# Gates of one token block added into DRAM by indirect transfers in place of one-hot products

## What is computed

```python
q = (h @ w_q).reshape(B, T, 8, 2, 128)               # 8 heads, two halves
s = einsum('bthpd,hpnd->bthpn', q, sub_keys)         # 128 keys for each half
v1, i1 = top_k(s[..., 0, :], 16); v2, i2 = top_k(s[..., 1, :], 16)
cand = v1[..., :, None] + v2[..., None, :]
top_s, pos = top_k(cand, 16)                         # 16 experts of 128*128 a head
eidx = i1 * 128 + i2 at pos
gates = softmax(top_s)
act = gelu(h . u_tab[eidx]);  out = sum(gates * act * v_tab[eidx])
```

## Time and profile before

| | |
|---|---|
| Three runs | 1858.15, 1858.62, 1856.65 us, median 1858.15 us |
| Profiled execution | span 1856.8 us from the first to the last instruction; no other time of it is listed |
| Busy | PE 95%, PEld 84%, DVE 70%, ACT 40%, POOL 41% of the span |
| Granted clock of TensorE | 0.981 of full speed on average |
| Transfers | 432.64 MB, 232 GB/s over the span |

### The profile page before, as it was taken

The page is one execution under the profiler, slowest core; times in us unless marked ns, Lnnn a source line. Parts: engine busy times, 40 slices in busy tenths (PEclk is TensorE's granted clock), DMA queues, the critical chain, the costliest instruction groups (busy, mean ns, idle before and its releaser), DMA issues. The chain is left out here.

```text
span 1856.8 us, 31058 instructions
## 1 busy us (share of the span) xinstructions
PE 1768.2 (95%) x11485; PEld 1564.7 (84%) x11485; DVE 1307.3 (70%) x2777; ACT 742.8 (40%) x1227; POOL 764.5 (41%) x449
## 2 busy tenths in 40 slices
PE   3999999999998989999999999879999999999998
PEld 2666888878877889999999999879998888888887
DVE  5993454553224679878869999756787888777777
ACT  4332332242234233333337767633333333333334
POOL 2333232344442448777753333122454443332330
PEclk9998999999999999999999999989999999999999
DMA  9661101022322249888868999978899999889883
GB/s 356 217 233 71 36 16 34 25 91 91 102 79 103 91 141 314 282 292 292 286 235 281 341 311 331 319 264 285 287 317 337 370 370 359 326 320 328 316 325 145
DMA packets 179267, 432.64 MB, mean 233 GB/s; under 512 B 15816, under 2 KB 91720, under 8 KB 179040
## 3 DMA queue, kind: packets, MB, share of 16 engines
q1 hardware_dynamic: 125088, 273.71, 42.5%
q0 software_dynamic: 36864, 134.23, 20.3%
q10 hardware_dynamic: 17216, 23.36, 3.4%
HBM read 383.54 MB, written 47.71 MB: 232 GB/s over the span
## 5 line engine op out<-in xcount | busy, mean ns | idle before, releaser
L201 POOL DMA_INDIRECT own_rows<-in_peer_v_dram,own_row x128 | 212.3, 1659 | 330.8 <-DVE y_own L2094 312.7
L1988 PE MATMUL banks<-v_hi,coef_lo 128*128 128x512 f32 x756 | 294.6, 390 | 0.0
L1988 PE MATMUL banks<-v_lo,coef_hi 128*128 128x512 f32 x756 | 294.5, 390 | 0.0
L1988 PE MATMUL banks<-v_hi,coef_hi 128*128 128x512 f32 x756 | 294.1, 389 | 0.1
L201 POOL DMA_INDIRECT own_rows<-in_u_rows_dram,own_row x128 | 160.6, 1255 | 233.1 <-DVE own_rows L1733 178.8
L2079 DVE TENSOR_TENSOR v_lo<-weight_ring,v_hi 128x1024 fp32r<-128x1024 f32 x128 | 156.5, 1222 | 24.7 <-ACT v_hi L2027 22.7
L1988 PEld LDWEIGHTS banks<-v_hi,coef_hi 128*128 128x128 f32 x756 | 142.0, 188 | 29.5 <-issue 0.5
L1988 PEld LDWEIGHTS banks<-v_hi,coef_lo 128*128 128x128 f32 x756 | 141.9, 188 | 29.5
L1988 PEld LDWEIGHTS banks<-v_lo,coef_hi 128*128 128x128 f32 x756 | 141.9, 188 | 28.9
L2094 DVE SCALAR_TENSOR_TENSOR y_own<-own_rows,own_coef,y_own 128x1024 f32<-128x1024 f32 x128 | 163.8, 1279 | 1.9 <-DVE y_own L2094 0.5
L1397 PE MATMUL banks<-h_hi,wring_hi 128*128 128x384 f32 (+2 forms) x448 | 155.2, 347 | 4.0 <-ACT gelu_early L1479 2.9
(11 more groups left out here) (393 smaller groups left out, 4346.1 us busy)
## 6 DMA issues: line engine op xcount, KB each, us to landing
weight_ring<-in_peer_v_dram SPq DMA_DIRECT2D x128, 512.0 KB, 5.4
weight_ring<-in_peer_u_dram SPq DMA_DIRECT2D x68, 512.0 KB, 4.5
ada<-in_w_ada_dram SPq DMA_DIRECT2D x48, 512.0 KB, 5.7
gate_scratch<-gate_block SPq DMA_DIRECT2D x48, 512.0 KB, 7.0
gate_tiles<-gate_scratch SPq DMA_DIRECT2D x32, 768.0 KB, 6.9
gelu_scratch<-gelu_early ACTq DMA_DIRECT2D x104, 192.0 KB
gelu<-gelu_scratch SPq DMA_DIRECT2D x104, 192.0 KB, 5.6
u_early<-in_peer_u_dram SPq DMA_DIRECT2D x36, 512.0 KB, 7.1
```

The lines of the kernel that those rows point to most:

```text
L201: pool.indirect_dma_start(own_rows[:, n % R], None, tables[n // NS], bass.IndirectOffsetOnAxis(ap=own_row[:, n % NS:n % NS + 1], axis=0)). ...
L1988: last = nc.tensor.matmul(y_bank(t, half)[:], w[:, j, t * P:(t + 1) * P], x[:, j, c], start=(first and n == 0), stop=False)
```

## The change

NSC = 1 of the three dense blocks no longer goes through one-hot products; only NHOT = 256 tokens do (HOT_TILES = 2), in NR = 4 turns. For the third block, VectorE works out for each head the 16 gates of a token (`list_gates`: softmax of that head alone, ScalarE's Exp by `add_exp`) and the place of each in the gates' DRAM tensor; GpSimd adds each into that place by an indirect transfer with 128 indices, one element of 4 bytes each (`add_gates`): 16 transfers a head, 128 in all. The tensor's part is zeroed before, by eight stores of SP in the DeltaNet stage. A head's adds wait until all of the head before have landed. Heads 0 to 5 are added during heads 2 to 7 of the search, two adds after each piece; heads 6 and 7 at the start of the one-hot stage, ahead of the fetches. In the search VectorE makes every second low part of the u pieces (`dve_split`), there are 4 dots a head, not 8, the loop over the heads is unrolled, and GpSimd fetches one row for two pieces. The expert stage has 36 u tiles, not 24, and 192 own rows, not 144.

```diff
+NSC = 1
+NHOT = TD - NSC * P
+HOT_TILES = NHOT // P
+NR = NHOT // (2 * TB)
-DOT_HEAD, DOT_ITER = 8, 8
+DOT_HEAD, DOT_ITER = 4, 8
-OWN_GELU = 8
+OWN_GELU = 22
+ZERO_PARTS = 8
...
-    if p < OWN_GELU:
-        return 2
-    if p == OWN_GELU:
-        return 0
+    if p < OWN_GELU - 1:
+        return 3
+    if p <= OWN_GELU:
+        return OWN_GELU - p
     if p < EXP_TILES - N_EARLY:
-        return 2 + (j > 0)
+        return 3
     if i >= 30:
         return int(j < 3)
-    return 0 if j == 0 else 1 if j < 3 else 1 + (i < 14)
+    return int(p > EXP_TILES - N_EARLY)
...
+                def add_gates(pool, h, n):
+                    if n == 0:
+                        pool.wait_ge(add_ready, h + 1)
+                        pool.wait_ge(gates_added, 16 * NSC * TOPK * h) if h else pool.wait_ge(gates_zeroed, 16 * ZERO_PARTS)
+                    t, k = n // TOPK, n % TOPK
+                    pool.indirect_dma_start(gates_at, bass.IndirectOffsetOnAxis(ap=add_at[:, h, t, k:k + 1], axis=0),
+                                            add_gate[:, h, t, k:k + 1], None, compute_op=ALU.add).then_inc(gates_added, 16)
...
                 nc.vector.memset(eps[:], EPS).then_inc(*V.step("eps"))
+                nc.vector.memset(g["zeros"][:], 0.0).then_inc(g["zeros_made"], 1)
...
+                    if i < ZERO_PARTS:
+                        sp.dma_start(spill[:, c, NHOT // TB:].rearrange("p g o j t -> p g (o j t)"),
+                                     g_["zeros"][:].unsqueeze(1).to_broadcast([P, EXP_TILES // G // ZERO_PARTS, NSC * G * P])).then_inc(g_["gates_zeroed"], 16)
...
+        def dve_split(n):
+            return n >= B0 + HR and (n - B0 - HR) % 2 == 1
...
+                def add_exp(h):
+                    act.wait_ge(*VB.after("add_shift", h))
+                    nc.scalar.activation(add_gate[:, h], add_gate[:, h], ACT.Exp).then_inc(add_exped, 1)
...
-                        if m == U_HEAD // 2 - 1 and h + 1 < PH:
-                            copy(h + 1)
+                        if m == U_HEAD // 2:
+                            if h + 1 < PH:
+                                copy(h + 1)
+                            if h:
+                                add_exp(h - 1)
+                add_exp(PH - 1)
...
-                n = R
-                for m in range(PH * U_HEAD):
-                    while n - R < (m + 1) * DOT_HEAD // U_HEAD:
-                        fetch(pool, n)
-                        n += 1
-                    if B0 + HR + m < NPIECE:
-                        rest(B0 + HR + m)
+                for h in range(PH):
+                    for m in range(U_HEAD):
+                        k = h * U_HEAD + m
+                        if k % 2:
+                            fetch(pool, R + k // 2)
+                        if B0 + HR + k < NPIECE and not dve_split(B0 + HR + k):
+                            rest(B0 + HR + k)
+                        if h >= 2:
+                            for n in range(m * NSC * TOPK // U_HEAD, (m + 1) * NSC * TOPK // U_HEAD):
+                                add_gates(pool, h - 2, n)
...
+                def list_gates(h):
+                    i1, i2 = (sel[:, n, SC, h, :] for n in range(2))
+                    total, inv, base, column = add_sum[:, 0], add_sum[:, 1], add_tmp[:, 0], add_tmp[:, 1]
+                    dve.wait_ge(add_exped, h + 1)
...
+                for h in range(PH):
+                    def fill(i):
+                        if i % 3 == 0:
+                            rest(B0 + HR + h * U_HEAD + 2 * (i // 3) + 1)
+                        if i in (1, 4, 7, 8):
+                            dot(h * DOT_HEAD + (1, 4, 7, 8).index(i))
+                        if i == 7 and h:
+                            list_gates(h - 1)
+                    topk(VB, h, DENSE, fill)
                 dve.wait_ge(*VB.after("sel1", PH - 1))
-                shift(VP, 0, ND)
-                softmax(VP, 0, ND, th(gates[:, 0:ND]), "gates")
+                shift(VP, 0, HOT_TILES)
+                list_gates(PH - 1)
+                softmax(VP, 0, HOT_TILES, th(gates[:, 0:HOT_TILES]), "gates")
...
                 pool.sem_inc(gelu_done, 2)
+                for h in (PH - 2, PH - 1):
+                    for n in range(NSC * TOPK):
+                        g_["add_gates"](pool, h, n)
                 for n in range(PH * DOT_HEAD + R, U_DONE + R):
                     fetch(pool, n)
```

More of the change, by code:

```diff
@@ L166, in program @@
             env["zT"] = sb(mix, "zT", [P, HJ, T])
+            env["zeros"] = sb(mix, "zeros", [P, NSC * G * P])
+            env["zeros_made"] = sem(mix, "zeros_made")
             env["scT"] = sb(mix, "scT", [P, HJ, T])
@@ L1457, in _ @@
                     pe.wait_ge(*(VB.after("sel1", PH - 1) if n < 2 else VP.after("gates")))
-                    for t in range(ND):
+                    for t in range(HOT_TILES):
                         src = (sel[:, n, t] if n < 2 else gates[:, t]).rearrange("p h k -> p (h k)")
@@ L1659, in _, with dot @@
                 dve.wait_ge(*VO.after("h_own"))
[L1661 to L1668 removed]
+                def dot(n):
+                    dve.wait_ge(row_landed[n % R], 16 * (n // R) + 16)
+                    nc.vector.scalar_tensor_tensor(rows[:, n % R], rows[:, n % R], 1.0, h_psum[:], ALU.mult, ALU.mult,
+                                                   accum_out=own_act[:, n:n + 1]).then_inc(row_used, 1)
@@ new lines, in rest @@
+                def rest(n):
+                    if n < NPIECE:
+                        dve.wait_ge(hi_ready, n + 1)
+                        nc.vector.tensor_tensor(w_lo[n % HR][:], w[:, n % WR], w_hi[n % HR][:].bitcast(F32), ALU.subtract).then_inc(lo_by_dve, 1)
+                def list_gates(h):
+                    i1, i2 = (sel[:, n, SC, h, :] for n in range(2))
+                    total, inv, base, column = add_sum[:, 0], add_sum[:, 1], add_tmp[:, 0], add_tmp[:, 1]
+                    dve.wait_ge(add_exped, h + 1)
+                    nc.vector.tensor_reduce(total, add_gate[:, h], AX.X, ALU.add).then_inc(*VS.step("sum"))
+                    dve.wait_ge(*VS.after("sum", h))
+                    nc.vector.reciprocal(inv, total).then_inc(*VS.step("inv"))
+                    nc.vector.tensor_copy(add_q[:], i2).then_inc(*VS.step("i2"))
+                    dve.wait_ge(*VS.after("i2", h))
+                    nc.vector.tensor_scalar(add_q[:], add_q[:], 2, None, ALU.logical_shift_right).then_inc(*VS.step("group"))
+                    for n in range(NSC):
+                        last = nc.vector.tensor_scalar(base[:, n], i1[:, n], float(ROW_P), lanes[:, n:n + 1], ALU.mult, ALU.add)
+                    last.then_inc(*VS.step("base"))
+                    dve.wait_ge(*VS.after("base", h))
+                    nc.vector.scalar_tensor_tensor(column, i2, float(TB), base, ALU.mult, ALU.add).then_inc(*VS.step("column"))
+                    dve.wait_ge(*VS.after("column", h))
+                    nc.vector.scalar_tensor_tensor(add_at[:, h], add_q[:], float(ROW_G - G * TB), column, ALU.mult, ALU.add).then_inc(*VS.step("at"))
+                    nc.vector.tensor_tensor(add_gate[:, h], add_gate[:, h], inv.unsqueeze(2).to_broadcast([P, NSC, TOPK]), ALU.mult).then_inc(*VS.step("gate"))
+                    dve.wait_ge(*VS.after("gate", h))
+                    dve.sem_inc(add_ready, 1)
@@ new lines, in _ @@
+                for n in range(NSC):
+                    nc.vector.tensor_scalar(lanes[:, n:n + 1], C["lane"][:, 0:1], float((HOT_TILES + n) * P * G), None, ALU.add).then_inc(lanes_ready, 1)
+                dve.wait_ge(lanes_ready, NSC)
+                for h in range(PH):
[7 more added lines that the diff above has]
+                    topk(VB, h, DENSE, fill)
@@ L1676, in _ @@
                 dve.wait_ge(turned, 3)
-                nc.vector.tensor_copy(gateT[:, 0:TD], bank[4][:, 0:TD]).then_inc(*VP.step("gT"))
+                nc.vector.tensor_copy(gateT[:], bank[4][:, 0:NHOT]).then_inc(*VP.step("gT"))
                 dve.wait_ge(*VP.after("gT"))
```

62 lines of the change are left out of this document (43 added, 19 removed).

## The result

The kernel after takes **1948.86 us** (median of four runs, 1945.23 to 1950.44), the kernel before 1857.97 us in the same comparison: ratio 1.049 with a 95% interval of 1.0475 to 1.0505. The forecast was 1895 us with a range of 1842 to 1935. The direction was right; the loss is 90.9 us, not 37, and the time lies outside the range.

A forecast was written before the change was run, and what follows sets the result against it. TensorE, busy 95% of the span, was taken as the bound. Span 1856.8 - 28.3 (turns) + 27 (search) + 4.5 (junction) + 34 (scatter's start) = 1894.0, so 1895 us; own range 1868 to 1928, 8 in 10 within 1842 to 1935.

The forecast's parts named there:

- the price of an add: GpSimd's time per 128-index adding transfer, taken as a row gather's: 1.25 us, 0.94 of instruction and 0.30 between.
- rival (c): An adding transfer costs clearly more than a gather: about 2015 us at 2.15, about 1935 at 1.6; chance 0.12.
- Search: Search stage: GpSimd needs 40.0 us a head against 34.6, in six heads with adds; 27 us lost.
- the junction: End of the search: VectorE's last selections, list_gates(7) and softmax bring the gates late; TensorE loses about 4.5 us.
- The stall at the scatter's start: One-hot stage's start: 32 adds ahead of own row 36's fetch hold up VectorE's fifth dot; 34 us lost, bounds 27 and 40.
- The fetch and its landing: One-hot stage's start: own row 36 takes 6.3 us to be fetched and land, after the 32 adds.
- the landing between the heads: One-hot stage's start: the first add of head 7 waits 3.3 us for the last of head 6.
- The landing at a head's end: Search: a head's first add waits for the previous head's last to land, one low part between; 2 us or more.
- The meetings of GpSimd and VectorE: VectorE's two-SBUF-operand work delays GpSimd: about 1 us for each of four low parts a head, about 8 at the stall.
- two turns out and twelve products in: One-hot loop two turns shorter, 78.5 us; 12 u products move to the expert stage, 50.2 us; net gain 28.3 us.
- The zeros: DeltaNet stage: one memset and eight 1 MB stores fit into idle time and cost nothing; 36 us without cover.
- VectorE's own low parts: Search: four low parts a head at 1.22 us bring VectorE to 28.8 of 34.6 us; enough by itself, no loss.

The follow-up runs named there:

- experiments 3 and 4: The kernel after with its 128 adds replaced: by plain 4-byte writes without adding, 1899.49 us; by gathers of 4 bytes per index, nothing written, 1896.12 us.
- Experiment 7: As experiment 6, but nine u tiles a head in place of eight and 28 u products in the expert stage; 1854.11 us, ratio 0.9983 to before.
- experiment 3: The kernel after with the same 128 indirect transfers writing their element in place of adding it; 1899.49 us.
- experiment 2: The kernel after without the 128 adds and the waits for their landing, all else kept; 1843.01 us, ratio 0.990 to before.
- experiment 8: As Experiment 7, with GpSimd's fetches at both ends of a head and two adds first in the one-hot stage; 1840.66 us, ratio 0.9901 to before.
- experiment 6: The kernel after with all search low parts on VectorE, fetches and adds mixed in the one-hot stage, list_gates(7) behind its first unit; 1859.91 us.

## Why the prediction was right in kind and wrong in size

**The step that failed is the price of an add**: "I take 1.25, as both build one transfer per index." It is 1.86 (1.56 of instruction, 0.30 between). The reason given was sound for what it named, as experiments 3 and 4 show at 0.97 and 0.95 us; it left out that adding costs GpSimd another 0.6 us. What came is rival (c), to which the forecast gave 0.12. Its sum there is also wrong: by its own formulas a price of 1.6 gives a head of 46.8 us, 68 us lost in the search and 45 at the stall, 1948 and not "about 1935". So the upper bound of 1935 left room for a price of about 1.5 only. The same 0.61 us counts twice:

- *Search.* 16 x 0.61 = 9.8 us more a head. Forecast 40.0 a head, measured 45.8, since 34.0 + 9.8 leaves 2.0 for the landing and the meetings, for which 6 had been set: two adds 0.8 us longer beside VectorE's low parts, and no wait for a landing. So the 6 were too much by 4, which hides a part of the price: with them, the head would be 49.8. Over six heads 45.8 turns 27 into 62 us; measured 63.9 without the junction.
- *The stall at the scatter's start.* 32 x 0.61 = 19.5 more: 34 would be 53.5. The fetch and its landing took 4.6 instead of 6.3, the landing between the heads 2.0 instead of 3.3, and the meetings 3.1 instead of about 8: together 7.9 less, which leaves 45.6. TensorE lost 47.1.

**The landing at a head's end** was put at 2 us from gathers that land 4.3 us after their issue. The only wait of this kind in the profile after is the 2.32 us one shown above, with nothing between two heads' adds: 3.9 us from the start of the last add. The 4.3 had been counted from the gather's start, though the low part only begins when the instruction is over; with it in between no wait is left. Experiment 7 shows the term to be real where the cover is gone.

The Trainium skill, "DMA: Bandwidth & Descriptors", section "Anatomy of one DMA — SWDGE (gpsimd) path", gives a fixed 2.0 us. The trace after comes near to it if one counts from the end of the add's instruction, 2.32 us; from its start it is the 3.9. It doesn't hold in every place here: 3.44 us and once 8.2 in experiment 7, and 5.01 us behind plain writes in experiment 3.

**The meetings of GpSimd and VectorE** cost both. GpSimd's side was forecast at 1 us for each of four low parts and is 0.8 us for two of them. That VectorE waits too, which no row of before showed, is seen in its timeline after, where its low part takes 1.23 us alone and 3.46 beside GpSimd's, and an operation of 16 columns 3.51:

```profile
774.96 1.23 DVE L1738 TENSOR_TENSOR wring_lo<-weight_ring,wring_hi 128x1024 fp32r<-128x1024 f32 x1 [2.40 <-ACT wring_hi L1520]
...
776.86 3.51 DVE L1663 TENSOR_TENSOR add_gate<-top 128x16 f32<-128x16 f32 x1
...
789.01 3.46 DVE L1738 TENSOR_TENSOR piece_lo<-weight_ring,piece_hi 128x1024 fp32r<-128x1024 f32 x1
```

The Trainium skill, "SBUF — State Buffer", section "SBUF: two separate sides", states this for whole instructions in either order, and the two rows agree with it: they are 2.2 and 3.3 us longer than alone, and both end only once a low part of GpSimd is over (788.41 to 791.38, and one from 777.41 to 780.33). It cost TensorE nothing in this version, as VectorE had slack; all waits for its low parts are 0.9 us.

**Right**: two turns out and twelve products in (the expert stage +50.9 for 50.2 forecast, no gap in it; its windows still show TensorE full at 3 own rows a tile). The zeros at nothing: the first part isn't longer. The place of the stall, 20 us into the stage. That the search's loss shows as waits for GpSimd's low parts, with VectorE's head filled but not over. **Right by luck**: the junction, 4.5 forecast and 4.3 measured. The forecast's own times, 44.4 and 38.8, are 5.6 apart, and the junction costs 6.2 us in experiment 2, where GpSimd doesn't hold the search up. **Left over**: the one-hot stage is 3.7 us longer than -78.5 + 47.1 says. Most of that is the clock: in the window from 1080 to 1120 us, which holds most of the long wait, it is 0.61, and behind the wait it is 0.50 until 1110 us, so that the 16 one-hot products of unit 5 take 3.79 us where they took 1.95 before; at the stage's start it is 0.50 until 1036 us. Of this the forecast had 2 us for the restart within its 34. And VectorE's own low parts, put at nothing, cost 5.7 us once GpSimd is fast (experiment 2).

```profile
1080.00:1120.00 40.00, 12.39 (x72) 12.39 (x73) 16.87 (x36) 3.61 (x6) 26.06 (x18) 0.61 0.57 139
```

**Is it the adds, or where they stand?** In experiment 8 an add is dearer still, 1.97 us on average without the gap, and yet the kernel gains 18.0 us over before, as much as the one without adds (15.7; the intervals overlap). The loss of the kernel after so lies in what else waits in GpSimd's queue: low parts that TensorE needs, and one fetch behind 32 adds. What the adds still cost in experiment 8 isn't shown, since no run leaves them out there. The books of experiment 8 against before, in spans: -78.5 for two turns, +33.4 for eight products in the search, +16.7 for four in the expert stage, +2.8 for the wait at the stage's end (4.5 for 1.7), +1.7 for the gates at the junction, and some 8 in the one-hot stage (185.1 for the 176.7 that four turns leave), of which 4.8 are waits for VectorE's one-hot tiles, make -15.5; measured -16.2.

## What to carry to other kernels

Before an engine's queue is given work of a new kind, price that kind by an experiment or leave its range open upward: with a count of 128, 0.61 us an instruction is 78 us, and a neighbour that does almost the same thing (here a gather for an add) bounds it from below only. Cheap work that nobody waits for must not stand in front of work that TensorE waits for: moving the low parts and the fetches out from behind the adds, and the last head's list of gates out of the junction, was worth 89 us with all the adds still there (experiment 6 against after), and with longer heads and the landing covered 108 us (experiment 8). And when such a delay seems cured, look at the place where all engines meet: the same lateness comes back there as one long wait (28.9 us in experiment 6), until the pace of the queue itself fits.

## What the runs showed of the hardware that had not been expected

- On GpSimd, away from VectorE's work, an indirect transfer with 128 indices takes 0.94 to 0.97 us whether it fetches 4 KB rows, fetches 4 bytes or writes 4 bytes; one that adds takes 1.55. The gap of 0.30 us behind each is the same.
- An add beside VectorE's three one-hot operations with two SBUF operands takes up to 3.83 us.
- GpSimd waited 5.01 us for the landing of 16 plain writes and 2.32 us for that of 16 adds, at the same place of the program, one wait of each. The writes also follow one another faster, 1.27 us apart and not 1.86; which of the two makes the difference was not separated.
- TensorE stays full while the DMA share is 1.01 and 385 GB/s are moved. The window of experiment 7 from 1500 to 1700 us:

```profile
1500.00:1700.00 200.00, 200.00 (x884) 165.57 (x883) 178.11 (x209) 72.34 (x98) 98.86 (x62) 1.00 1.01 385
```
